# Turning q and the attention's probabilities on VectorE instead of TensorE

## The chip, the cores and the metric

The kernel runs on one core of a Trainium2 chip, in one launch. The metric is device microseconds of an execution. All operands are float32; the products run on values split into two float32r parts.

## The reference

A block with three residual steps on x of 256 tokens by 2048: half a SwiGLU FFN (width 5632), a mixer, and again half a SwiGLU FFN, with an RMSNorm ahead of each and one at the end. The mixer projects to 5376 columns and has two groups of heads:

```python
p = h @ w_in                       # q of 16 heads x 64, k and v of 2 heads x 64, retention's q, k, v, gate
logits = einsum('bnqhgd,bnkhd->bnhgqk', qc, kb) * 64 ** -0.5   # chunks of 64 queries, windows of 128 keys
probs = softmax(concat([logits, sink], -1))[..., :-1]
out = einsum('bnhgqk,bnkhd->bnqhgd', probs, vb)
x = x + concat(out, retention) @ w_out
```

## The kernel before

**Tiling.** The products are weight streams: a weight matrix goes by in groups of 2048 rows by 512 columns (4 MB). A group is eight *halves*; a half is 256 rows, and TensorE computes it in `half` (line 357) as 12 products of 128x512: two row tiles, two token tiles, and three terms each, hi*hi, hi*lo and lo*hi. SP loads 1 MB of weights (two halves) at a time into one of four slots of `raw`. ScalarE copies a half from `raw` into `w_hi` (rounded, line 694), VectorE subtracts to get `w_lo` (line 914). This is a *split*; there are four slots of each, so that a split is made four halves ahead: `position(g, k)` on ScalarE and VectorE is the split of half k + 4, ScalarE's waits until TensorE has finished half k (`half_used`), VectorE's waits for ScalarE's, and TensorE's half waits for VectorE's (`lo_ready`).

**Order.** Every engine runs an order written out by hand; what isn't weight work is put between positions k by `if k == ...`. The input projection has 11 column blocks of up to 512. Two of them, 16 halves, are a *pair*. TensorE's `pair(i, quad)` numbers its halves (e, k) with e = 0, 1 and k = 0 to 7; ScalarE's and VectorE's `in_pair(i, j)` count k = 0 to 15. Pair 0 gives k, v and the first columns of q. The four pairs after it are a loop (`Fori`) in which the attention runs beside the projection, one *quad* (four heads, two token tiles) a pair. The attention is one chain through the engines:

1. GpSimd's `stage` copies the quad's q out of `proj` into `q_in` (line 1207), and k and v into `kT` and `v`; this happens during the quad before.
2. After half 1 TensorE turns q by eight transposes into PSUM (line 392 for every transpose); ScalarE copies to `qT` (line 806).
3. After half 3 the logits (line 512), 32 small products.
4. VectorE takes the maximum in position 3, ScalarE the exponentials into `probs` in position 4 (line 814).
5. After half 8, (1, 0), TensorE turns the probabilities by eight transposes; ScalarE and VectorE copy one bank each to `probsT` (lines 822 and 1101).
6. After half 10, (1, 2), the weighing with v (`weigh`, line 525); VectorE scales by the denominators in position 10 (line 1105), TensorE turns the result after half 13, and both parts of `attT` are made in position 13.

GpSimd, after the last quad's logits, rotates retention's q and k in 24 instructions of 128x512 (`rotate`, lines 1228 to 1235); their scratch is `q_in` and `qT`.

The FFN turns its hidden tile h on VectorE already, by instructions of 32 partitions (`turn_h`, line 983):

```python
out = ps[dst * SQ:(dst + 1) * SQ, B_DOWN:B_DOWN + 2, :].rearrange(
    "p b (j t c) -> p t (b j) c", j=2, t=T)[:, :, :, src * SQ:(src + 1) * SQ]
blocks = h[src * SQ:(src + 1) * SQ, :, :].rearrange(
    "p t (k c) -> p t k c", k=4)[:, :, :, dst * SQ:(dst + 1) * SQ]
m = dve.transpose(out, blocks)
```

Of the kernel before, what the change touches and what calls it, by code (L numbers as in the profile page):

```python
# [20 lines left out]
P = 128  # L21
D = 2048
SEQ = 256
T = SEQ // P
# [9 lines left out]
HD = 64  # L34
KV = 2
QUAD = 4
# [50 lines left out]
def build(nc, x_d, xT_d, g1, u1, d1, w_in, sinks_d, gn_d, w_out, g2, u2, d2, fw_d, ident_d, cos_d, sin_d,  # L87
          decay_d, out_d):
    ffn_w = [(g1, u1, d1), (g2, u2, d2)]
    with ExitStack() as ctx:  # L90
# [3 lines left out]
        def sem(name):  # L94
            return ctx.enter_context(nc.semaphore(name))
# [113 lines left out]
        q_in_ready = sem("q_in_ready")  # L209
        kT_in_ready = sem("kT_in_ready")  # L210
        v_in_ready = sem("v_in_ready")
        q_turned = sem("q_turned")
        qT_ready = sem("qT_ready")
        logits_ready = sem("logits_ready")
        soft = sem("soft")
# [1 line left out]
        sink_m_ready = sem("sink_m_ready")  # L217
        probs_ready = sem("probs_ready")
        sink_e_ready = sem("sink_e_ready")
        probs_turned = sem("probs_turned")  # L220
        probsT_a = sem("probsT_a")
        probsT_b = sem("probsT_b")
        pv_done = sem("pv_done")
        att_ready = sem("att_ready")
        att_turned = sem("att_turned")
# [128 lines left out]
        def _(pe):  # L354
# [160 lines left out]
                mm.then_inc(logits_ready, 1)  # L515

            def weigh(quad):
                pe.wait_ge(probsT_a, quad)
                pe.wait_ge(probsT_b, quad)
                pe.wait_ge(v_in_ready, quad)  # L520
                for t in range(T):
                    for hh in range(QUAD):
                        for c in range(2):
                            col = (t * QUAD + hh) * HD
                            mm = pe.matmul(ps[c * CH:(c + 1) * CH, B_DOWN + 2, col:col + HD],  # L525
                                           probsT[:, t, hh * P + c * CH:hh * P + (c + 1) * CH],
                                           v[:, t, c, :], start=True, stop=True)
                mm.then_inc(pv_done, 1)

            def in_projection():  # L530
                def pair(i, quad=None):
                    for e in range(2):
                        pe.wait_ge(proj_ready, 2 * i + (e + 1))
                        for k in range(8):
                            if quad is None and e == 0:
                                pe.wait_ge(xT_lo_ready, PAIRS * MIX + k + 1)
                            if quad is not None and (e, k) == (0, 3):
                                pe.wait_ge(attT_lo_ready, quad)
                            half(2 * i + (G_IN + e), k, xT_hi, xT_lo, 2 * k, B_GATE + 2 * e, k == 0, k == 7)
                            if quad is None and (e, k) == (1, 2):  # L540
                                pe.wait_ge(proj_ready, 2 + 1)
                                for g in range(KV):
                                    for t in range(T):
                                        mm = turn(B_DOWN, (g * T + t) * P,
                                                  proj[:, t, A_K + g * HD:A_K + (g + 1) * HD])
                                mm.then_inc(k_turned, 1)
                            if quad is not None and (e, k) == (0, 1):
                                pe.wait_ge(kT_ready, 3)
                                pe.wait_ge(q_in_ready, quad)
                                for t in range(T):  # L550
                                    for hh in range(QUAD):
                                        mm = turn(B_DOWN + t, hh * P, q_in[:, t, hh * HD:(hh + 1) * HD])
                                mm.then_inc(q_turned, 1)
                            if quad is not None and (e, k) == (0, 3):
                                logits(quad)
                            if quad is not None and (e, k) == (1, 0):
                                pe.wait_ge(probs_ready, quad)
                                for t in range(T):
                                    for hh in range(QUAD):
                                        mm = turn(B_DOWN + t, hh * P, probs[:, t, hh, :])  # L560
                                mm.then_inc(probs_turned, 1)
                            if quad is not None and (e, k) == (1, 2):
                                weigh(quad)
                            if quad is not None and (e, k) == (1, 5):
                                pe.wait_ge(att_ready, quad)
                                for k2 in range(2):
                                    for t in range(T):
                                        mm = turn(B_DOWN + 3, k2 * SEQ + t * P, att[:, t, k2 * P:(k2 + 1) * P])
                                mm.then_inc(att_turned, 1)

                pair(0)
                with pe.Fori(1, NQ + 1) as quad:
                    pair(quad, quad)
                pe.wait_ge(proj_ready, 2 + NI - 2)
                for k in range(8):
                    half(G_OUT - 1, k, xT_hi, xT_lo, 2 * k, B_GATE, k == 0, k == 7, W_LAST)
# [86 lines left out]
        def _(act):  # L663
# [131 lines left out]
            def in_pair(i, j=None):  # L795
                for k in range(16):
                    position(2 * i + G_IN, k)
                    if k == 7:
                        proj_out(2 * i, B_GATE)
                    if k == 15:  # L800
                        proj_out(2 * i + 1, B_UP)
                    if j is None:
                        continue
                    if k == 1:
                        act.wait_ge(q_turned, j + 1)
                        act.activation(qT.rearrange("p t c -> p (t c)"),
                                       ps[0:HD, B_DOWN:B_DOWN + 2, :].rearrange("p t c -> p (t c)"),
                                       ACT.Copy).then_inc(qT_ready, 1)
                    if k == 4:
                        act.wait_ge(neg_m_ready, j + 1)  # L810
                        for t in range(T):
                            for hh in range(QUAD):
                                c = t * QUAD + hh
                                a = act.activation(probs[:, t, hh, :], ps[:, B_DOWN + 2 + t, hh * P:(hh + 1) * P],
                                                   ACT.Exp, bias=neg_m[:, c:c + 1], scale=HD ** -0.5,
                                                   accum_out=den[:, c:c + 1])
                        a.then_inc(probs_ready, 1)
                        act.wait_ge(sink_m_ready, j + 1)
                        act.activation(sink_e[:], sink_m[:], ACT.Exp).then_inc(sink_e_ready, 1)
                    if k == 8:  # L820
                        act.wait_ge(probs_turned, j + 1)
                        act.activation(probsT[:, 0, :], ps[:, B_DOWN, :], ACT.Copy).then_inc(probsT_a, 1)
                    if k == 13:
                        act.wait_ge(att_turned, j + 1)
                        act.activation(attT_hi[:, bass.ds(2 * j, 2), :], ps[:, B_DOWN + 3, :].rearrange(
                            "p (k s) -> p k s", k=2), ACT.Copy).then_inc(attT_hi_ready, 1)
# [81 lines left out]
        def _(dve):  # L908
# [149 lines left out]
            def weigh_final(t, n):  # L1058

                cols = slice(n * W, (n + 1) * W)  # L1060
                if t == 0 and n < ND - LATE:
                    dve.wait_ge(x_added, X_FFN[1] + 4 * (NF - 1) + n + 1)
                dve.tensor_tensor(normed[:, t, cols], x[:, t, cols], final_w[:, cols],
                                  ALU.mult).then_inc(x_weighted, 1)

            def in_pair(i, j=None):
                for k in range(16):
                    position(2 * i + G_IN, k)
# [7 lines left out]
                                        turned[:, :, 0, CH:2 * CH]).then_inc(kT_ready, 1)  # L1076
                    if j is None:
                        continue
                    if k == 3:

                        dve.wait_ge(logits_ready, j + 1)
# [10 lines left out]
                        dve.wait_ge(neg_m_ready, j + 1)  # L1092
                        dve.tensor_tensor(sink_m[:], sinks[:, bass.ds(8 * j, 8)], neg_m[:],
                                          ALU.add).then_inc(sink_m_ready, 1)
                    if k == 8:
                        dve.wait_ge(sink_e_ready, j + 1)
                        dve.tensor_tensor(den2[:], den[:], sink_e[:], ALU.add).then_inc(soft, 1)
                        dve.wait_ge(soft, 4 * j + 3)
                        dve.reciprocal(rden[:], den2[:]).then_inc(soft, 1)
                        dve.wait_ge(probs_turned, j + 1)  # L1100
                        dve.tensor_copy(probsT[:, 1, :], ps[:, B_DOWN + 1, :]).then_inc(probsT_b, 1)
                    if k == 10:
                        dve.wait_ge(pv_done, j + 1)
                        dve.wait_ge(soft, 4 * j + 4)
                        dve.tensor_tensor(att[:].rearrange("p t (h d) -> p (t h) d", h=QUAD),
                                          ps[:, B_DOWN + 2, :].rearrange("p (h d) -> p h d", d=HD),
                                          rden[:].unsqueeze(2).to_broadcast([P, T * QUAD, HD]),
                                          ALU.mult).then_inc(att_ready, 1)
                    if k == 13:
                        dve.wait_ge(attT_hi_ready, j + 1)  # L1110
                        dve.tensor_tensor(attT_lo[:, bass.ds(2 * j, 2), :],
                                          ps[:, B_DOWN + 3, :].rearrange("p (k s) -> p k s", k=2),
# [81 lines left out]
        def _(pool):  # L1194
# [5 lines left out]
            def stage(j):  # L1200

                again = not isinstance(j, int)
                if again:
                    pool.wait_ge(proj_ready, j + (2 + 1))
                    pool.wait_ge(q_turned, j)
                    pool.wait_ge(v_in_ready, j)
                pool.tensor_copy(q_in[:], proj[:, :, bass.ds(j * QUAD * HD + A_Q, QUAD * HD)]).then_inc(q_in_ready, 1)
                if again:
# [118 lines left out]
```

## Time and profile before

| | us |
|---|---|
| median of 3 runs (lowest, highest) | 1819.68 (1819.52, 1819.89) |
| the profiled execution | 1819.52 |
| its span, first to last instruction | 1817.7 |
| busy: TensorE products / weight loads | 1806.8 / 1495.2 |
| busy: VectorE / ScalarE / GpSimd | 1184.4 / 824.7 / 63.9 |

The span is what the trace shows; 1.8 us of the execution lie around it. Busy time sums the instructions of an engine. A product's record (0.39 us for 128x512) is longer than the distance to the next one, since they are pipelined; for TensorE read distances between starts.

### The profile page before, as it was taken

Reading aid. Unit: us, or ns where it says so; the run is one execution under the profiler, and the core shown is the slowest. Engines: PE = TensorE matmul, PEld = TensorE weight load, DVE = VectorE, ACT = ScalarE, POOL = GpSimd, SP = SyncE. Lnnn points to the kernel's source line nnn. Section 1 sums busy time; section 2 is a strip of 40 time slices with the busy share of each in tenths; the row PEclk is TensorE's granted clock in tenths of the full one; section 3 lists DMA queues with packets and bytes.
Section 4 is the critical chain, followed back from the end, with each engine's and each line's share of the span. In section 5 each row is a group of like instructions: output and inputs, shape, how many; then the busy total and the mean of one; then the engine's idle time right before and its main releaser. Section 6 shows DMA issues by size and latency. Waiting matters only on the chain.

```text
span 1817.7 us, 22705 instructions
## 1 busy us (share of the span) xinstructions
PE 1806.8 (99%) x8308; PEld 1495.2 (82%) x8308; DVE 1184.4 (65%) x1403; ACT 824.7 (45%) x990; POOL 63.9 (4%) x60
## 2 busy tenths in 40 slices
PE   9999999999999999999999999999999999999998
PEld 7888888888888888888888888888888888888886
DVE  6676676676666667544467665676676666667666
ACT  6434444443443444555555455444443443444444
POOL 0000000000000000100045000000000000000000
PEclk9999999999999999999999999999999999999999
DMA  9566566566555555554545456565566555565562
GB/s 384 197 192 201 185 194 198 185 197 195 186 199 192 187 203 186 168 181 163 174 149 185 139 186 208 185 195 198 186 196 196 186 199 192 188 200 190 189 204 93
DMA packets 175587, 346.64 MB, mean 191 GB/s; under 512 B 5952, under 2 KB 8640, under 8 KB 175424
## 3 DMA queue, kind: packets, MB, share of 16 engines
q1 hardware_dynamic: 174976, 345.35, 57.6%
q10 hardware_dynamic: 576, 0.81, 0.1%
q8 instruction: 23, 0.38, 0.1%
q14 instruction: 12, 0.10, 0.0%
HBM read 344.04 MB, written 2.10 MB: 190 GB/s over the span
## 4 chain that ended last, share of the span: by engine, by line
PE 98%; DVE 1%; issue 0%; ACT 0%; DMA 0%; SPq 0%; POOLq 0%; POOL 0%; DVEq 0%; ACTq 0%
PE ps L363 32%; PE ps L365 32%; PE ps L364 32%; PE ps L392 1%; DVE w_lo L914 0%; PE ps L512 0%; DMA raw<-in_g 0%; PE ps L600 0%; PE ps L611 0%; PE ps L525 0%; ACT w_hi L671 0%; ACT w_hi L694 0%; PE ps L481 0%; PE ps L479 0%; PE ps L480 0%
## 5 line engine op out<-in xcount | busy, mean ns | idle before, releaser
L914 DVE TENSOR_TENSOR w_lo<-raw,w_hi 128x1024 fp32r<-128x1024 f32 x644 | 801.3, 1246 | 596.3 <-ACT w_hi L694 595.2
L694 ACT ACTIVATE w_hi<-raw 128x1024 fp32r<-128x1024 f32 x644 | 682.9, 1061 | 962.4 <-PE ps L365 954.1
L363 PE MATMUL ps<-w_hi,xT_hi 128*128 128x512 f32 (+1 forms) x1808 | 703.7, 389 | 1.2 <-DVE w_lo L914 1.1
L365 PE MATMUL ps<-w_hi,xT_lo 128*128 128x512 f32 (+1 forms) x1808 | 700.3, 387 | 0.0
L364 PE MATMUL ps<-w_lo,xT_hi 128*128 128x512 f32 (+1 forms) x1808 | 700.3, 387 | 0.0
L363 PEld LDWEIGHTS ps<-w_hi,xT_hi 128*128 128x128 f32 x1808 | 339.5, 188 | 71.9 <-DVE w_lo L914 1.6
L365 PEld LDWEIGHTS ps<-w_hi,xT_lo 128*128 128x128 f32 x1808 | 339.5, 188 | 69.7
L364 PEld LDWEIGHTS ps<-w_lo,xT_hi 128*128 128x128 f32 x1808 | 339.6, 188 | 68.3
L363 PE MATMUL ps<-w_hi,hT_hi 128*128 128x512 f32 x640 | 249.1, 389 | 0.0
L365 PE MATMUL ps<-w_hi,hT_lo 128*128 128x512 f32 x640 | 249.0, 389 | 0.0
L364 PE MATMUL ps<-w_lo,hT_hi 128*128 128x512 f32 x640 | 249.0, 389 | 0.0
L983 DVE STREAM_TRANSPOSE ps<-h 32x256 f32<-32x256 f32 x320 | 146.0, 456 | 7.1
L365 PEld LDWEIGHTS ps<-w_hi,hT_lo 128*128 128x128 f32 x640 | 120.1, 188 | 25.0
L363 PEld LDWEIGHTS ps<-w_hi,hT_hi 128*128 128x128 f32 x640 | 120.1, 188 | 24.9
L364 PEld LDWEIGHTS ps<-w_lo,hT_hi 128*128 128x128 f32 x640 | 120.1, 188 | 24.8
L999 DVE SCALAR_TENSOR_TENSOR x<-ps,x 128x512 f32<-128x512 f32 x188 | 120.4, 682 | 0.1
L1197 POOL TENSOR_TENSOR rstd<-ms_eps,minus_half 128x2 f32<-128x2 f32 (+1 forms) x5 | 3.2, 641 | 1491.8 <-DVE ms_eps L958 1491.8
L363 PE MATMUL ps<-w_hi,attT_hi 128*128 128x512 f32 x112 | 45.5, 406 | 0.0
L365 PE MATMUL ps<-w_hi,attT_lo 128*128 128x512 f32 x112 | 43.8, 391 | 0.0
L364 PE MATMUL ps<-w_lo,attT_hi 128*128 128x512 f32 x112 | 43.6, 390 | 0.0
L968 DVE SCALAR_TENSOR_TENSOR h<-ps,rstd,sg 128x512 f32<-128x512 f32 x44 | 30.9, 743 | 0.0
L733 ACT ACTIVATE sg<-ps,rstd 128x512 f32<-128x512 f32 x44 | 27.4, 673 | 0.0
(117 smaller groups left out, 522.2 us busy)
## 6 DMA issues: line engine op xcount, KB each, us to landing
raw<-in_u SPq DMA_DIRECT2D x88, 1024.0 KB, 5.1
raw<-in_d SPq DMA_DIRECT2D x88, 1024.0 KB, 4.9
raw<-in_g SPq DMA_DIRECT2D x85, 1024.0 KB, 5.1
raw<-in_w_in SPq DMA_DIRECT2D x40, 1024.0 KB, 4.9
raw<-in_w_out SPq DMA_DIRECT2D x16, 1024.0 KB, 4.9
raw<-in_g SPq DMA_DIRECT2D x4, 512.0 KB, 7.4
x<-in_x SPq DMA_DIRECT2D x4, 512.0 KB, 12.9
raw<-in_w_in SPq DMA_DIRECT2D x4, 512.0 KB, 3.6
```

Of the source, the lines that this page charges most:

```text
L363: pe.matmul(out, xh, wh, start=first and j == 0, stop=False)
L364: pe.matmul(out, xh, wl, start=False, stop=False)
L365: mm = pe.matmul(out, xl, wh, start=False, stop=last and j == 1)
L392: return pe.transpose(ps[0:src.shape[1], bank, col:col + P], src, ident[:])
L694: act.activation(dst, raw[:, s, (k % 2) * HALF:(k % 2 + 1) * HALF], ACT.Copy).then_inc(hi_ready, 1)
L733: act.activation(sg[:, t, :], ps[:, B_GATE + t, :], ACT.Silu, scale=rstd[:, (FFN1, FFN2)[f], t:t + 1]).then_inc(silu_done, 1)
L914: dve.tensor_tensor(w_lo[:, k % LEAD, :, :].rearrange(flat), raw[:, k // 2, (k % 2) * HALF:(k % 2 + 1) * HALF], f32(w_hi[:, k % LEAD, :, : ...
L968: dve.scalar_tensor_tensor(out=h[:, t, :], in0=ps[:, B_UP + t, :], scalar=rstd[:, (FFN1, FFN2)[f], t:t + 1], in1=sg[:, t, :], op0=ALU.mult ...
L983: m = dve.transpose(out, blocks)
L999: a = dve.scalar_tensor_tensor(out=xb, in0=ps[:, B_DOWN + 2 * (n % 2) + t, :], scalar=scale, in1=xb, op0=ALU.mult, op1=ALU.add)
L1197: pool.tensor_tensor(rstd[:, norm, t0:t1], ms_eps[:, norm, t0:t1], minus_half[:, t0:t1], ALU.pow).then_inc(rstd_ready, 1)
```

## The change

Per quad, q is turned by eight and the probabilities by sixteen VectorE transposes, each of which takes 32 partitions by 256 elements (eight blocks of 32x32) from one group of 32 partitions of the source and writes them to a group of `qT` or `probsT`. TensorE's sixteen transposes, ScalarE's copies to `qT` and `probsT` and VectorE's to `probsT` go. Three transposes follow each of VectorE's positions 0 and 1, two position 2 (q), four follow positions 6 and 7, three 8 and 9, two 10 (probabilities). On TensorE the weighing moves from after half 10 to after half 11 and the turn of its result from half 13 to half 14; VectorE's denominators move from position 8 to 11, the scaling from 10 to 12, the making of `attT` from 13 to 14. GpSimd's next `q_in` waits for `qT_ready` where it waited for `q_turned`.

```diff
@@ TensorE
             def weigh(quad):
-                pe.wait_ge(probsT_a, quad)
-                pe.wait_ge(probsT_b, quad)
+                pe.wait_ge(probsT_ready, quad)
@@
-                            if quad is not None and (e, k) == (0, 1):
-                                pe.wait_ge(kT_ready, 3)
-                                pe.wait_ge(q_in_ready, quad)
-                                for t in range(T):
-                                    for hh in range(QUAD):
-                                        mm = turn(B_DOWN + t, hh * P, q_in[:, t, hh * HD:(hh + 1) * HD])
-                                mm.then_inc(q_turned, 1)
                             if quad is not None and (e, k) == (0, 3):
                                 logits(quad)
-                            if quad is not None and (e, k) == (1, 0):
-                                pe.wait_ge(probs_ready, quad)
-                                for t in range(T):
-                                    for hh in range(QUAD):
-                                        mm = turn(B_DOWN + t, hh * P, probs[:, t, hh, :])
-                                mm.then_inc(probs_turned, 1)
-                            if quad is not None and (e, k) == (1, 2):
+                            if quad is not None and (e, k) == (1, 3):
                                 weigh(quad)
-                            if quad is not None and (e, k) == (1, 5):
+                            if quad is not None and (e, k) == (1, 6):
                                 pe.wait_ge(att_ready, quad)
@@ ScalarE
-                    if k == 1:
-                        act.wait_ge(q_turned, j + 1)
-                        act.activation(qT.rearrange("p t c -> p (t c)"),
...
-                    if k == 8:
-                        act.wait_ge(probs_turned, j + 1)
-                        act.activation(probsT[:, 0, :], ps[:, B_DOWN, :], ACT.Copy).then_inc(probsT_a, 1)
-                    if k == 13:
+                    if k == 14:
                         act.wait_ge(att_turned, j + 1)
@@ VectorE
+            def turn_q(b0, b1):
+                for b in range(b0, b1):
+                    d, c = b // 4, b % 4
+                    to = qT_full[d * SQ:(d + 1) * SQ, :, :].rearrange("p t (h c) -> p t h c", h=QUAD)
+                    of = q_in[c * SQ:(c + 1) * SQ, :, :].rearrange("p t (h c) -> p t h c", h=QUAD)
+                    m = dve.transpose(to[:, :, :, c * SQ:(c + 1) * SQ], of[:, :, :, d * SQ:(d + 1) * SQ])
+                return m
+            def turn_probs(b0, b1):
+                for b in range(b0, b1):
+                    d, c = b // 4, b % 4
+                    to = probsT[d * SQ:(d + 1) * SQ, :, :].rearrange("p t (h c) -> p t h c", h=QUAD)
+                    of = probs[c * SQ:(c + 1) * SQ, :, :, :]
+                    m = dve.transpose(to[:, :, :, c * SQ:(c + 1) * SQ], of[:, :, :, d * SQ:(d + 1) * SQ])
+                return m
@@ in_pair
+                    if k == 0:
+                        dve.wait_ge(q_in_ready, j + 1)
+                    if k < 3:
+                        m = turn_q(3 * k, min(3 * k + 3, 8))
+                    if k == 2:
+                        m.then_inc(qT_ready, 1)
@@
-                    if k == 8:
+                    if k == 6:
+                        dve.wait_ge(probs_ready, j + 1)
+                    if 6 <= k < 11:
+                        m = turn_probs(*((0, 4), (4, 8), (8, 11), (11, 14), (14, 16))[k - 6])
+                    if k == 10:
+                        m.then_inc(probsT_ready, 1)
+                    if k == 11:
                         dve.wait_ge(sink_e_ready, j + 1)
...
-                        dve.wait_ge(probs_turned, j + 1)
-                        dve.tensor_copy(probsT[:, 1, :], ps[:, B_DOWN + 1, :]).then_inc(probsT_b, 1)
-                    if k == 10:
+                    if k == 12:
                         dve.wait_ge(pv_done, j + 1)
...
-                    if k == 13:
+                    if k == 14:
                         dve.wait_ge(attT_hi_ready, j + 1)
@@ GpSimd
-                    pool.wait_ge(q_turned, j)
+                    pool.wait_ge(qT_ready, j)
```

## Rows read from the trace of the kernel before

**Rows 1.** The page, chain that ended last: share of the span by engine.

```profile
PE 98%; DVE 1%; issue 0%; ACT 0%; DMA 0%; SPq 0%; POOLq 0%; POOL 0%; DVEq 0%; ACTq 0%
```

**Rows 2.** Waits, 770 to 970 us: engine, line, releaser; us in total, times, longest.

```profile
PEld ps L512 <- issue: 1.4, 4, 0.4
```

**Rows 3.** Windows, one pair: length, busy us (instructions) by engine, clock, DMA share, GB/s.

```profile
778.50:827.77 49.27, 49.27 (x278) 40.64 (x276) 23.48 (x25) 25.20 (x42) 3.66 (x3) 1.00 0.52 171
```

**Rows 4.** Timeline of PE in the first quad: start, length, engine, line, operation, operands.

```profile
778.49 0.40 PE L365 MATMUL ps<-w_hi,xT_lo 128*128 128x512 f32 x1
...
782.11 0.39 PE L365 MATMUL ps<-w_hi,xT_lo 128*128 128x512 f32 x1
...
784.83 0.39 PE L365 MATMUL ps<-w_hi,xT_lo 128*128 128x512 f32 x1
785.15 1.96 PE L512 MATMUL ps<-kT,qT 64*64 64x64 f32 x32
...
800.59 0.39 PE L365 MATMUL ps<-w_hi,xT_lo 128*128 128x512 f32 x1
...
804.21 0.39 PE L365 MATMUL ps<-w_hi,xT_lo 128*128 128x512 f32 x1
...
806.93 0.39 PE L365 MATMUL ps<-w_hi,xT_lo 128*128 128x512 f32 x1
807.25 1.15 PE L525 MATMUL ps<-v,probsT 128*64 128x64 f32 x32
```

**Rows 5.** VectorE in the FFN: group (count, busy us, mean ns), then its timeline.

```profile
L983 DVE STREAM_TRANSPOSE ps<-h 32x256 f32<-32x256 f32 x320 | 146.0, 456 | 7.1
...
301.01 1.23 DVE L914 TENSOR_TENSOR w_lo<-raw,w_hi 128x1024 fp32r<-128x1024 f32 x1 [1.49 <-ACT w_hi L694]
302.15 1.28 DVE L999 SCALAR_TENSOR_TENSOR x<-ps,x 128x512 f32<-128x512 f32 x2
...
314.70 1.23 DVE L914 TENSOR_TENSOR w_lo<-raw,w_hi 128x1024 fp32r<-128x1024 f32 x1 [0.38 <-ACT w_hi L694]
315.96 0.91 DVE L983 STREAM_TRANSPOSE ps<-h 32x256 f32<-32x256 f32 x2
```

**Rows 6.** Groups of VectorE by shape: two-input and one-input work within SBUF.

```profile
L1063 DVE TENSOR_TENSOR proj<-x,proj 128x512 f32<-128x512 f32 x8 | 5.3, 689 | 0.2
...
L1190 DVE TENSOR_SCALAR proj<-proj,rstd 128x512 f32<-128x512 f32 x3 | 1.3, 484 | 0.7 <-POOL rstd L1197 0.7
```

**Rows 7.** Timelines of ACT and DVE at the head of the first quad's pair.

```profile
776.27 1.28 ACT L694 ACT_TABLE_LOAD   x1 [0.58 <-PE ps L365]
...
778.93 1.06 ACT L694 ACTIVATE w_hi<-raw 128x1024 fp32r<-128x1024 f32 x1 [0.30 <-PE ps L365]
...
778.66 2.59 DVE L914 TENSOR_TENSOR w_lo<-raw,w_hi 128x1024 fp32r<-128x1024 f32 x2 [2.86 <-ACT w_hi L694]
```

**Rows 8.** Timelines of ACT and DVE around the first quad's probabilities.

```profile
798.30 1.06 ACT L694 ACTIVATE w_hi<-raw 128x1024 fp32r<-128x1024 f32 x1 [1.66 <-PE ps L365]
...
801.02 1.06 ACT L694 ACTIVATE w_hi<-raw 128x1024 fp32r<-128x1024 f32 x1 [0.51 <-PE ps L365]
...
796.68 1.22 DVE L914 TENSOR_TENSOR w_lo<-raw,w_hi 128x1024 fp32r<-128x1024 f32 x1 [0.30 <-ACT w_hi L694]
799.39 1.23 DVE L914 TENSOR_TENSOR w_lo<-raw,w_hi 128x1024 fp32r<-128x1024 f32 x1 [1.49 <-ACT w_hi L694]
```

**Rows 9.** The last quad: line 914 (min/median/max ns), then DVE, POOL and PE timelines.

```profile
L914 DVE TENSOR_TENSOR w_lo<-raw,w_hi x7: 1257/2002/2360, 939.2 to 956.3; 128x1024 fp32r<-128x1024 f32 x7
...
943.00 6.46 DVE L914 TENSOR_TENSOR w_lo<-raw,w_hi 128x1024 fp32r<-128x1024 f32 x3 [1.48 <-ACT w_hi L694]
...
944.00 2.16 POOL L1228 TENSOR_TENSOR q_in<-proj,sin 128x512 f32<-128x512 f32 x1
...
955.09 1.15 PE L525 MATMUL ps<-v,probsT 128*64 128x64 f32 x32
```

**Rows 10.** Timeline of PE: its first instructions of the run.

```profile
1.46 3.60 PE L625 MATMUL ps<-junk 128*128 128x512 bf16 x8 [1.46 <-DVE junk L1116]
```

More of the change, by code:

```diff
@@ L211, in build @@
         v_in_ready = sem("v_in_ready")
-        q_turned = sem("q_turned")
         qT_ready = sem("qT_ready")
@@ L219, in build @@
         sink_e_ready = sem("sink_e_ready")
-        probs_turned = sem("probs_turned")
-        probsT_a = sem("probsT_a")
-        probsT_b = sem("probsT_b")
+        probsT_ready = sem("probsT_ready")
         pv_done = sem("pv_done")
@@ L803, in in_pair @@
                         continue
-                    if k == 1:
-                        act.wait_ge(q_turned, j + 1)
-                        act.activation(qT.rearrange("p t c -> p (t c)"),
-                                       ps[0:HD, B_DOWN:B_DOWN + 2, :].rearrange("p t c -> p (t c)"),
-                                       ACT.Copy).then_inc(qT_ready, 1)
                     if k == 4:
```

## The prediction

> **What bounds the kernel now.** I read the chain of waits first: 98% of what ended last is TensorE [rows 1]. Then the waits of the stage that the change touches: no other engine holds TensorE there, only its own issue, as the 1.4 us ahead of the four quads' logits [rows 2]. Then the same stage by windows: one pair of column blocks lasts 49.27 us and TensorE is busy for all of it at granted clock 1.00 (2.4 GHz), while VectorE is busy for 23.48 us and ScalarE for 25.20 us [rows 3]. So an instruction taken from TensorE is worth its full time, and one added to VectorE is free only until TensorE waits for its result.
>
> **What TensorE gives back.** A half is 12 products of 128x512. An undisturbed one goes from 782.11 to 784.83, 2.72 us. The half before it, with the eight transposes of q in front, goes from 778.49 to 782.11, 3.62 us: 0.90 us for the eight and the disturbance behind them. The probabilities' eight: 800.59 to 804.21, 3.62 us, again 0.90 us, and the half after it 2.72 us [rows 4]. 2 x 0.90 = 1.80 us a quad, 7.2 us for four quads. ScalarE also loses two copies and VectorE one; both were behind work that nobody waited for, so I count them at nothing.
>
> **What VectorE gets: the price of one transpose.** The trace has the same instruction, 32x256 float32, but from SBUF into PSUM: 456 ns, 320 times [rows 5]; the new ones write SBUF. Bounds: a two-input SBUF instruction of 128x512 takes 689 ns and a one-input one 484 ns [rows 6], so one-input SBUF work can stream two elements a cycle of about 1.04 ns. If the new transposes did, 256 elements would cost 133 ns less. From above, 484 ns is 267 ns of that faster streaming and 217 ns fixed, and 217 + 267 for 256 elements at one a cycle is again 484 ns. I take 456 ns, the same operation, and keep 0.32 and 0.484 us as ends.
>
> How closely they follow each other matters as much. A split of 128x1024 (record 1.23 us) is followed by an ordinary instruction after 1.14 us (301.01 to 302.15), but by a transpose that goes to other partitions after 1.26 us (314.70 to 315.96), and a pair of transposes takes 0.91 us, twice 456 ns with no overlap [rows 5]. So 0.456 us each in a chain, against 0.34 us if starts overlapped by the same 0.12 us.
>
> The Trainium skill, "VectorE: DVE Perf Modes", section "Two Vector instructions with no wait between them", has this as a rule: an instruction whose input or output starts in another group of 32 partitions than the last one is held until all earlier ones have finished. The trace agrees (1.26 against 1.14 us); by the rule nearly all 24 new transposes and the splits behind them are held, and without it they would not be, which is a rival below. The same page, section "The three transpose paths", gives 311 ns for a 128x128 bf16 transpose into SBUF; an estimate from it for twice the elements, at 0.96 GHz, is 311 + 133 = 444 ns, by which the sum below would be about 0.8 us smaller.
>
> **The q turn: does it fit?** Position k of VectorE is the split for the half four later; it needs ScalarE's w_hi, whose start VectorE's follows by 1.09 us (798.30, 799.39 [rows 8]). At the loop's head ScalarE reloads its table (1.28 us at 776.27), so VectorE's position 0 starts late, at 778.66, and position 1's input is there at 778.93 + 1.09 = 780.02 [rows 7]. Now the new queue: split at 778.66, first transpose after 1.14 (it stays on the first partitions), three of 0.456 end at 781.17; split 1.26 and three more end at 783.80; split 1.26 and two end at 785.97. Every split's input is there before its turn. TensorE reached the logits at 785.15 [rows 4]; without the q turn it is there at 784.25. It waits 1.72 us plus 0.1 us for signal and start (my estimate): 1.8 us a quad, twice what the q transposes gave back. Behind the waiting TensorE stands half 4, then everything. ScalarE and the DMAs only follow; weight loads have the lead of four halves, 10.9 us. VectorE's next work, position 3 and the maximum, waits for the logits anyway, and GpSimd's q_in copy, now released by the same signal, falls beside that split: nothing for either.
>
> **The probabilities' turn.** Times as in the trace before, counted from the logits. Position 6 starts at 796.68 [rows 8], the exponentials being done. +1.14 and four transposes: 799.64. Position 7's input was there at 799.39; 1.26 + 1.82: 802.72. Position 8's (801.02 + 1.09 = 802.11) is there; 1.26 + 1.37: 805.35. Positions 9 and 10 are also late by VectorE itself: +1.26 + 1.37 = 807.98, +1.26 + 0.91 = 810.15. TensorE weighed at 807.25, after half 10; now it does so after half 11 and without the turn: 807.25 - 0.90 + 2.72 = 809.07. Wait: 1.08 + 0.1 = 1.2 us a quad. The VectorE copy and den2/rden moved to position 11 lie behind it; att at 12 and its turn after half 14 keep over 1 us of room; no w_lo is late, since half 11's is made at 800.9 for a start at about 806.
>
> **The last quad.** Once its logits are done GpSimd rotates, 24 instructions on end. There the splits take 2.00 us in the median and three in a row 6.46 us, and GpSimd's instructions 2.16 us where they meet one [rows 9]. Two-input SBUF instructions of both take turns; the transposes have one input, and I leave them at 0.456. Position 5 ends at 943.00 + 2.15 = 945.15; five splits of 2.00 and 16 transposes are 17.3 us: 962.45. TensorE is there at 955.09 - 0.90 + 2.72 = 956.91, counted in the same way. Wait: 5.5 + 0.1 = 5.6 us in place of 1.2.
>
> **Sum.** -7.2 + 4 x 1.8 + 3 x 1.2 + 5.6 = +9.2 us. The profiled execution took 1819.52 us (span 1817.7), 0.16 below the median of 1819.68. Forecast 1819.5 + 9.2 = 1828.7 us, 0.5% slower. Its own range: transposes of 0.484 add 2.7 us, five splits of 2.36 (the longest of that row [rows 9]) 1.8; gentler turns with GpSimd take off up to 4.4.
>
> **Rivals.**
> 1. GpSimd doesn't lengthen the last turn (the transposes let it run in their time): the last wait is 1.2 us too, +4.8 us, 1824.3. For it: GpSimd's instructions alone are short; against it: it has 24 of them in a row, so some one is under way whenever a split comes.
> 2. The starts overlap (no hold): 0.34 us each. q wait 0.9; the second is then paced by ScalarE, about 0.35; the last 945.15 + 10.0 + 5.4 + 0.1 - 956.9 = 3.8. -7.2 + 3.6 + 1.05 + 3.8 = +1.2 us: 1820.7, no change. Against it: the 1.26 us of rows 5.
> 3. The other side: transposes from SBUF to SBUF stream two elements a cycle and overlap, 0.34 - 0.13 = 0.21 us. Then VectorE has q ready at about 784.3 and the probabilities at 809.1, waits of 0.1 us, and the last about 1.5 us: -7.2 + 0.4 + 0.3 + 1.5 = -5.0 us, 1814.5. It decides from the spacing below which the waits sum to under 7.2 us, about 0.32 us. For it: the 484 ns of rows 6; against it: 456 ns in 320 transposes, though none of them could show it, having PSUM as target.
> 4. The clock. It is 1.00 through this stage before [rows 3], but TensorE never idles there. The first eight 128x512 products of the run, after nothing, take 3.60 us, 0.42 us apart [rows 10], where 0.227 is the spacing at 2.4 GHz: the lower level, 1.2 GHz. If the last wait of 5.6 us brings it back for as many products, that is 8 x 0.2 = 1.6 us more, 1830.3. The Trainium skill, "TensorE: Matmul & The Clock Gate", section "Why this matters for your kernels", warns of this for idle gaps; no row here shows it.
>
> **Chances.** Forecast 0.46, with the clock's extra 0.09, rival 1 0.2, rival 2 0.12, rival 3 0.08, something else 0.05. The likeliest one's time is the prediction. The range 1820.3 to 1833.5 holds rivals 1, 2 and 4 and the dearer transposes. 0.2% (3.6 us) is about what a measurement of this kernel can tell from no change. Slower: forecast, clock and rival 1 save a small part of it, 0.73; the same: rival 2 and that part, 0.16; faster: rival 3 and half of the rest, 0.11.
>
> **What would show it.** TensorE waits ahead of the logits, named VectorE, four times 1.8 us; ahead of weigh, 1.2 us three times and over 4 us in the last quad; pairs of 49.27 - 1.80 + 3.0 = 50.5 us; new transposes of 440 to 485 ns, back to back; clock 1.00 but for the last quad. I am wrong if the transposes are under 0.35 us apart, if a w_lo is waited for, or if the waits are there but TensorE's transposes had cost less than 0.90 us a turn.

## The result, and the profile after

The changed kernel takes 1834.27 us (median of 4, 1830.99 to 1836.11) against 1819.79: ratio 1.0078, 95% interval 1.0064 to 1.0091. It is slower by 14.5 us; the forecast of 1828.7 us is 8.9 above this median, and the upper end of its range, 1833.5, was passed by 0.8 us. The profiled execution took 1834.15 us, span 1832.3.

The chain that ended last, against [rows 1]: TensorE has lost three parts in a hundred of it to VectorE and to "issue".

```profile
PE 95%; DVE 2%; issue 2%; ACT 0%; POOLq 0%; POOL 0%; DVEq 0%; ACTq 0%
```

Who waited for whom, 770 to 990 us, against [rows 2] (engine, line waited; us in total, times, longest; PEld is the weight load that waits, PE the product behind it; line 509 is the logits, 521 weigh, 1054 the transposes of the probabilities):

```profile
PEld ps L521 <- DVE probsT L1054: 9.9, 4, 5.8
PEld ps L509 <- issue: 8.2, 4, 2.1
PE ps L521 <- DVE probsT L1054: 8.2, 4, 5.4
PE ps L509 <- issue: 6.7, 4, 1.7
```

Both waits of the prediction are there, four times each: up to 1.7 us ahead of each logits, and ahead of weigh 0.94 us three times and 5.4 once. The one ahead of the logits is called "issue": this view doesn't name its releaser, and the timeline of VectorE has to be laid beside it. The timeline of TensorE in the first quad, against [rows 4], and in the last, against [rows 9]:

```profile
783.96 0.39 PE L362 MATMUL ps<-w_hi,xT_lo 128*128 128x512 f32 x1
786.01 0.65 PE L509 MATMUL ps<-kT,qT 64*64 64x64 f32 x12 [1.66 <-issue]
```

```profile
809.56 0.39 PE L362 MATMUL ps<-w_hi,xT_lo 128*128 128x512 f32 x1
810.88 0.80 PE L521 MATMUL ps<-v,probsT 128*64 128x64 f32 x20 [0.94 <-DVE probsT L1054]
```

```profile
966.42 0.39 PE L362 MATMUL ps<-w_hi,xT_lo 128*128 128x512 f32 x1
972.16 1.12 PE L521 MATMUL ps<-v,probsT 128*64 128x64 f32 x16 [5.35 <-DVE probsT L1054]
```

VectorE at the head of the first quad, against [rows 7]:

```profile
778.69 1.23 DVE L889 TENSOR_TENSOR w_lo<-raw,w_hi 128x1024 fp32r<-128x1024 f32 x1 [2.86 <-ACT w_hi L677]
779.83 1.32 DVE L1046 STREAM_TRANSPOSE qT<-q_in 32x256 f32<-32x256 f32 x3
781.16 1.23 DVE L889 TENSOR_TENSOR w_lo<-raw,w_hi 128x1024 fp32r<-128x1024 f32 x1
782.42 1.33 DVE L1046 STREAM_TRANSPOSE qT<-q_in 32x256 f32<-32x256 f32 x3
783.76 1.23 DVE L889 TENSOR_TENSOR w_lo<-raw,w_hi 128x1024 fp32r<-128x1024 f32 x1
785.02 0.89 DVE L1046 STREAM_TRANSPOSE qT<-q_in 32x256 f32<-32x256 f32 x2
```

The queue is the one that was worked out: the last q transpose ends at 785.91 (785.97 was forecast) and the logits start at 786.01. The new transposes against [rows 5]:

```profile
L1054 DVE STREAM_TRANSPOSE probsT<-probs 32x256 f32<-32x256 f32 x64 | 27.9, 436 | 1.1
...
L1046 DVE STREAM_TRANSPOSE qT<-q_in 32x256 f32<-32x256 f32 x32 | 13.9, 434 | 0.5
```

436 and 434 ns, 0.02 us less than those into PSUM, one behind the other without overlap (three in 1.32 to 1.33 us), and 1.26 us from a split's start to a first transpose that goes to other partitions, 1.14 to one that doesn't. That is the hold of [rows 5].

What the forecast lacks stands in the windows (length, busy us of PE, clock, DMA share, GB/s) behind the second quad's q wait:

```profile
836.00:838.00 2.00, 1.82 (x26) 0.70 0.56 216
838.00:840.00 2.00, 2.00 (x12) 0.50 0.63 136
840.00:842.00 2.00, 2.00 (x7) 0.50 0.99 386
842.00:844.00 2.00, 2.00 (x7) 0.60 0.01 2
844.00:846.00 2.00, 2.00 (x11) 1.00 0.00 0
```

The granted clock falls to 0.50, the 1.2 GHz level, while the logits run behind the 1.66 us of idleness (their 32 small products have 64x64 on one side and 64 or 128 columns on the other), and is back at 2.4 GHz before 844. Products are then 0.43 us apart in place of 0.227:

```profile
840.26 0.63 PE L362 MATMUL ps<-w_hi,xT_lo 128*128 128x512 f32 x1
840.69 0.63 PE L360 MATMUL ps<-w_hi,xT_hi 128*128 128x512 f32 x1
```

**The account**, by the start of the first logits product and of the first weigh product in each quad. The column on the right is the run fill, described below, whose TensorE has work in the waits. Undisturbed, logits to weigh would be 22.10 - 0.90 + 2.72 = 23.92 us.

| us | before | after | after, TensorE kept busy (fill, below) |
|---|---|---|---|
| logits to weigh, quad 1 | 22.10 | 24.87 | 24.90 |
| quad 2 | 22.10 | 28.07 | 24.89 |
| quad 3 | 22.10 | 26.47 | 24.90 |
| quad 4 | 22.10 | 30.86 | 29.49 |
| weigh to the next logits | 27.18 | 25.29 to 25.30 | 25.30 to 25.33 |
| last weigh to the retention's first transpose | 31.37 | 28.92 | 26.85 |

Weigh to logits is 27.18 - 2.72 - 0.90 + 1.74: the q wait is 1.74 us. The last line would be 31.37 - 2.72 = 28.65; fill has 1.8 us less, because the kernel before waited there and fill doesn't. The projection's last group is narrow (256 columns), its splits took turns with GpSimd's rotation, and TensorE waited for w_lo (kernel before, 965 to 1003 us, line 914):

```profile
PEld ps L363 <- DVE w_lo L914: 1.6, 3, 0.7
```

In the changed kernel and in fill the rotation, started by the logits, is over earlier against TensorE, which has waited ahead of weigh; that view of them has no such row. The changed kernel loses 28.92 - 26.85 = 2.07 us there all the same, at clock 0.50, which it reached within its last weigh wait of 5.35 us (0.50 from 970 on):

```profile
972.00:974.00 2.00, 1.84 (x32) 0.50 0.00 0
974.00:976.00 2.00, 2.00 (x9) 0.50 0.66 173
976.00:978.00 2.00, 2.00 (x9) 0.82 0.25 89
```

So: give-back -7.2; q waits 4 x 1.74 = 7.0; weigh waits 3 x 0.95 = 2.9; the last weigh wait 29.49 - 23.92 = 5.6; the clock, by the differences between after and fill, 3.18 + 1.57 + 1.37 + 2.07 = 8.2; the narrow group's wait -1.8. Sum +14.7; the spans differ by 14.6.

The four runs say the same by their mean clock: 1830.99 us at 0.996, 1834.15 and 1834.38 at 0.993, 1836.11 at 0.992. A varying number of falls would explain the scatter of 5 us in a kernel whose predecessor scatters by 0.6; only one of the four was profiled.

### The profile page after: what moved, and what is told of

Its sections match the earlier page's. It is cut to its first block, busy times and chain, and to the rows that moved or that the text cites. A ratio compares the mean times of both kernels' runs of the same rounds, so it can differ in the third digit from the quotient of the medians.

```text
span 1832.3 us, 22657 instructions
## 1 busy us (share of the span) xinstructions
PE 1807.8 (99%) x8244; PEld 1496.2 (82%) x8244; DVE 1217.2 (66%) x1495; ACT 819.0 (45%) x982; POOL 57.3 (3%) x60
## 4 chain that ended last, share of the span: by engine, by line
PE 95%; DVE 2%; issue 2%; ACT 0%; POOLq 0%; POOL 0%; DVEq 0%; ACTq 0%
PE ps L360 31%; PE ps L361 31%; PE ps L362 31%; DVE probsT L1054 1%; DVE w_lo L889 1%; PE ps L389 1%; PE ps L509 1%; PE ps L521 0%; ACT w_hi L677 0%; PE ps L583 0%; PE ps L594 0%; PE ps L380 0%; PE ps L376 0%; PE ps L384 0%; PE ps L608 0%
## 5 line engine op out<-in xcount | busy, mean ns | idle before, releaser
L1054 DVE STREAM_TRANSPOSE probsT<-probs 32x256 f32<-32x256 f32 x64 | 27.9, 436 | 1.1
```

The costliest lines, as they stand in the source:

```text
L1054: m = dve.transpose(to[:, :, :, c * SQ:(c + 1) * SQ], of[:, :, :, d * SQ:(d + 1) * SQ])
```

## The experiments

Theory: the 14.5 us are give-back, two waits and the clock falls behind them. Rivals: VectorE's work beside TensorE costs by itself; or the clock has another cause. Ratios are against the kernel before, whose median was 1819.6 to 1819.9 us beside these runs.

**q_only**: the probabilities' half of the change undone.

```diff
-                        m = turn_probs(*((0, 4), (4, 8), (8, 11), (11, 14), (14, 16))[k - 6])
...
+                            if quad is not None and (e, k) == (1, 0):
...
+                                        mm = turn(B_DOWN + t, hh * P, probs[:, t, hh, :])
...
```

> Only the q turn is VectorE's; the probabilities are turned by TensorE and weighed after half 10, as before. Theory (the waits, and clock falls behind the q waits): TensorE gives back 4 x 0.90 = 3.6 us and waits 4 x 1.73 = 6.9 us ahead of the logits, +3.3 us over the kernel before (1819.8), so 1823.1 at full clock; and 1.2 to 1.7 us more for each quad in which the clock falls behind the wait (in the changed kernel three of four), so about 1827 and a mean clock near 0.996. Rival (the clock falls behind the long last weigh wait or the number of VectorE transposes, not behind the q waits): 1823 with clock 0.999.

Measured 1828.60 us (1828.33 to 1829.86), ratio 1.0052 (1.0038 to 1.0066), clock 0.995. The same q waits, and the fall behind the second:

```profile
PEld ps L511 <- issue: 8.2, 4, 2.1
PE ps L511 <- issue: 6.6, 4, 1.7
```

```profile
832.00:842.00 10.00, 8.34 (x51) 0.75 0.62 208
842.00:852.00 10.00, 10.00 (x41) 0.91 0.01 2
```

Logits to weigh is 22.05, 25.28, 23.67 and 23.62 us: 3.2 + 1.6 + 1.5 us above 22.10. The falls belong to the q waits; the rival would have had 1823. The time is 1.6 us above the theory's 1827, since the falls cost 6.3 us together where it had at most 5.1. The account closes: -3.6 + 7.0 + 6.3, and -0.8 for the last weigh to the retention (30.56 us against 31.37), is +8.9.

**probs_only**: the q half undone.

```diff
-                        m = turn_q(3 * k, min(3 * k + 3, 8))
...
+                                        mm = turn(B_DOWN + t, hh * P, q_in[:, t, hh * HD:(hh + 1) * HD])
...
```

> Only the probabilities are VectorE's; q is turned by TensorE after half 1. Theory: -3.6 us, weigh waits of 0.95 us in three quads and about 5.2 in the last, +4.4 us: 1824.2 at full clock, with one fall, in the last quad behind its wait, 1.6 to 3 us more: 1825.8 to 1827, clock 0.998, and no fall at 1 us waits. Rival (falls come with VectorE's transposes beside TensorE anywhere): clock under 0.996 and over 1828.

Measured 1825.35 us (1824.81 to 1825.74), ratio 1.0031 (1.0019 to 1.0044), clock 0.997: the mechanism as the theory had it, the time 0.4 us under its range. Logits to weigh is 24.93 us in three quads, with no fall behind their waits, and 29.59 in the last, behind which the clock is 0.70 in the mean of 10 us. The halves, +8.9 and +5.6, add up to the +14.5. That is in part luck: their falls come to 8.5 us where the changed kernel's come to 8.2, and what they save in the narrow group to 2.6 where it saves 1.8.

**fill**: TensorE is kept busy in the waits. What the fillers compute is used by nobody.

```diff
+            def fill(n):
+                for _ in range(n):
+                    pe.matmul(ps[:, B_DOWN + 1, :], xT_hi[:, 0, 0:P], xT_hi[:, 0:2, :].rearrange("p k s -> p (k s)"),
+                              start=True, stop=True)
...
+                                fill(6)
                                 logits(quad)
...
+                                fill(20 if isinstance(quad, int) else 3)
                                 weigh(quad)
...
-                with pe.Fori(1, NQ + 1) as quad:
-                    pair(quad, quad)
+                with pe.Fori(1, NQ) as quad:
+                    pair(quad, quad)
+                pair(NQ, NQ)
```

> The changed kernel with products of x by itself into an unused bank ahead of each wait, 6 ahead of the logits (1.36 us of the 1.73 waited), 3 ahead of weigh, 20 in the last quad (4.5 us); their results are used by nobody. Theory: the waits end when they did, since VectorE sets their end, but TensorE isn't idle: clock back to 0.999 and the time to the sum of give-back and waits alone, 1819.8 - 7.2 + 6.9 + 2.9 + 5.2 = 1827.6. Rival (the clock isn't part of it, the 14.5 us are all waits): 1834 or, since the fillers add work, more.

Measured 1826.04 us (1825.78 to 1826.15), ratio 1.0035 (1.0021 to 1.0048), clock 0.999. More work on TensorE made it 8.2 us faster, and its runs agree within 0.4 us. The logits start at 786.01 and 836.24, where the changed kernel's do (786.01, 836.18): VectorE still sets them. TensorE's last pair also stands outside the loop here, for its 20 fillers; the second and third quads, in the loop in both kernels, lose their falls all the same (28.07 and 26.47 us against 24.89 and 24.90). The second quad's window in the changed kernel, then in fill:

```profile
822.00:872.00 50.00, 47.40 (x245) 38.75 (x244) 31.54 (x47) 22.12 (x38) 2.52 (x3) 0.93 0.50 166
```

```profile
822.00:872.00 50.00, 49.44 (x270) 40.58 (x269) 33.03 (x49) 23.65 (x40) 2.53 (x3) 1.00 0.50 168
```

The 8.2 us are the clock's share of the account, and all of it. It ended 1.6 us under the theory, which lacked the narrow group's wait (1.8 us) and had 5.2 for a last wait of 5.6.

**early_q**: the same eight transposes, in positions 11 to 15 of the pair before.

```diff
+                    if turn_next and k == 11:
+                        dve.wait_ge(q_in_ready, done + 1)
+                    if turn_next and k >= 11:
+                        m = turn_q(*((0, 2), (2, 3), (3, 5), (5, 6), (6, 8))[k - 11])
+                    if turn_next and k == 15:
+                        m.then_inc(qT_ready, 1)
...
-                    if k < 3:
-                        m = turn_q(3 * k, min(3 * k + 3, 8))
...
```

> The changed kernel with each quad's q turned one pair earlier, in VectorE's positions 11 to 15; same instructions, no wait at the logits. Theory: the 6.9 us of q waits and the falls behind them go; left are -7.2 + 2.9 + 5.2 = +0.9 us and one fall in the last quad, 1.6 to 3 us: 1822 to 1824, clock 0.998. Rival (VectorE's load beside TensorE costs, wherever it is put): over 1828.

Measured 1821.69 us (1821.00 to 1822.62), ratio 1.0011 (1.0002 to 1.0020), clock 0.997: 12.6 us back for moving eight instructions a quad, and 0.3 us under the theory's range. What is left ahead of the logits is the 1.4 us of issue of [rows 2]; weigh's waits stand:

```profile
PEld ps L521 <- DVE probsT L1054: 10.1, 4, 6.0
PE ps L521 <- DVE probsT L1054: 8.4, 4, 5.6
...
PEld ps L509 <- issue: 1.4, 4, 0.4
```

**early_q_alone**: q as in early_q, the probabilities as before.

> Only q is VectorE's, turned one pair earlier; the probabilities are turned by TensorE as before. Theory: half of the give-back and no wait, -3.6 us: 1816.1, clock 0.999. Rival (VectorE's eight transposes delay a w_lo or the give-back is less): 1818 or more.

Measured 1816.05 us (1815.76 to 1816.90), ratio 0.9981 (0.9972 to 0.9990): the half give-back to 0.1 us. Logits to weigh is 22.09 us, weigh to logits 26.28, that is 27.18 - 0.90: a turn costs TensorE 0.90 us, and eight transposes a quad beside it cost it nothing.

**late_rotate**: the changed kernel with GpSimd held until the last weighing.

```diff
-            pool.wait_ge(logits_ready, NQ)
+            pool.wait_ge(pv_done, NQ)
```

> The changed kernel, but GpSimd's rotation waits for the last quad's weighing instead of its logits. Theory: the last weigh wait shrinks from about 5.2 us to the 0.95 of the other quads, 4.2 us, and the one clock fall behind it goes, about 1.3 us: 1834.3 - 5.5 = 1828.8, clock 0.995, the q waits and their falls left. Rival (the last wait is long for another reason, or the rotation is then late for the retention): 1833 or more.

Measured 1833.79 us (1833.36 to 1835.39), ratio 1.0079 (1.0065 to 1.0092). The total is the rival's, though the last wait did shrink: its longest weigh wait is 1.4 us. Its clock falls ahead of weigh (26.43, 28.06, 26.47, 26.43 us from logits to weigh) are 7.9 us above four times 24.87, where the changed kernel has 6.1. Its trace also has two waits behind the last weighing that the changed kernel's lacks, 1.9 us for w_lo in and right behind the narrow group and 1.9 us for `att` in the retention. The next run has the same two, without clock falls.

**early_q_late_rotate**: early_q and late_rotate together.

> q turned one pair earlier and the rotation late; all 24 transposes a quad still VectorE's. Theory: left are the give-back and four weigh waits of 0.95 us, -7.2 + 3.8 = -3.4 us: 1816.3, clock 0.999, faster than the kernel before. Rival (transposes beside TensorE cost it something by themselves): 1818 or more.

Measured 1820.42 us (1819.97 to 1821.63), ratio 1.0006 (0.9997 to 1.0015), clock 0.999: not to be told from no change, and a miss by 4.1 us. The wait is gone as expected (early_q has 10.1 us, longest 6.0, in this row):

```profile
PEld ps L521 <- DVE probsT L1054: 5.4, 4, 1.4
```

Logits to weigh in the last quad is 24.91 us, as in the others, where early_q has 29.59: the last wait was GpSimd's doing, 4.7 us of it. The total is the rival's (1818 or more), its mechanism isn't: 24 transposes a quad run beside TensorE, and weigh to logits is 23.56 to 23.60 us where 27.18 - 2.72 - 0.90 = 23.56 was due. The gain was given back later: TensorE waits 1.9 us for w_lo in and right behind the narrow group (1.6 before, in the narrow group) and 1.9 us for `att` in the retention. The next run shows the second at its clearest.

**no_waits**: as the last one, and weigh after half 12.

```diff
-                            if quad is not None and (e, k) == (1, 3):
+                            if quad is not None and (e, k) == (1, 4):
                                 weigh(quad)
...
```

> As the one with early q and late rotation, and weigh one half later again (after half 12, the scaling in position 13, attT in 15): no wait left. Theory: the whole give-back, -7.2 us: 1812.5, clock 0.999. Rival (a dependent step of the last quad is then late, or the give-back was less than 0.90 us a turn): 1814 or more.

Measured 1821.12 us (1820.69 to 1821.86), ratio 1.0009 (0.9999 to 1.0018). A miss by 8.6 us, and the first half of the rival (a dependent step of the last quad is late) is what happened. No quad waits (26.64 us from logits to weigh, 23.92 + 2.72), but the retention does:

```profile
PE ps L389 <- ACT att L849: 4.4, 1, 4.4
PE ps L360 <- DVE w_lo L889: 2.3, 4, 0.6
```

`gn_rstd` is the scale of a retention head's norm, which GpSimd computes behind all four rotations in its order. GpSimd still rotates when the first head's is due; ScalarE's `att` waits for it, and TensorE waits 4.4 us for ScalarE. In that wait the clock falls, and it is 0.50 from 1002 to 1008. It is a new wait, made by my own edit.

**split_rotate**: the changed kernel with only heads 1 to 3 of the rotation held.

```diff
             for hd in range(RH):
+                if hd == 1:
+                    pool.wait_ge(pv_done, NQ)
                 rotate(hd)
```

> The changed kernel, with GpSimd rotating head 0 behind the last logits as it did, and heads 1 to 3 behind the last weighing. The late rotation of all four heads ended too late for the retention's first gn_rstd (TensorE waited there instead); this one should end some 8 us earlier. Theory: the last weigh wait becomes 0.95 us, its clock fall goes, no new wait: 1834.3 - 4.2 - 1.3 = 1828.8. Rival (the last wait isn't GpSimd's doing, or the retention waits anyway): 1833 or more.

Measured 1832.78 us (1831.08 to 1834.25), ratio 1.0069 (1.0056 to 1.0083). It missed by 4 us, at the edge of the rival's 1833: the four weigh waits are alike (5.4 us in all), but in the profiled execution the clock fell in every quad (28.10, 26.48, 26.47, 28.09 us from logits to weigh, 9.7 us above four times 24.87), and the narrow group waits again (1.7 us for w_lo). Where the q waits stand, a gain of 4 us can't be read from the total.

**split_no_waits**: early q, weigh after half 12, split rotation.

> q turned one pair earlier, weigh after half 12, and the rotation split in the same way. Theory: no wait at the logits, at weigh or in the retention: the whole give-back of 16 transposes a quad, 1819.6 - 7.2 = 1812.4, clock 0.999. Rival (GpSimd still ends too late, or transposes beside TensorE cost it something): 1815 or more.

Measured 1814.46 us (1814.04 to 1814.97), ratio 0.9970 (0.9959 to 0.9982), clock 0.999: the fastest, 5.4 us under the kernel before, of 7.2 expected. For the missing 1.8 us the trace shows GpSimd again: it rotates through the whole narrow group, nine splits take 19.59 us, 2.2 each, and TensorE's halves wait for w_lo (line 889). The median is under the rival's 1815. From weigh to the retention it is 27.07 us where 31.37 - 2 x 2.72 = 25.93 were to be had, and the retention's first head takes 0.7 us longer:

```profile
966.68 19.59 DVE L889 TENSOR_TENSOR w_lo<-raw,w_hi 128x1024 fp32r<-128x1024 f32 x9
```

```profile
PE ps L360 <- DVE w_lo L889: 2.0, 4, 0.6
```

## Why the prediction was wrong

- **Give-back, 7.2 us**: right. early_q_alone and the pairs of starts give 0.90 us a turn.
- **Price of a transpose, 0.456 us, held**: right in kind, 0.436 in size. (For 444 ns the prediction has the sum about 0.8 us smaller; 96 transposes of 12 ns less are 1.2 us, as its own 2.7 us for 484 ns is 96 times 28 ns.) The overlap of rival 2 and the doubled stream of rival 3 aren't there.
- **q wait, 1.8 us**: 1.74. **Weigh wait, 1.2 us**: 0.95, since the 16 transposes ahead of it are 20 ns shorter each. **The last one, 5.6 us**: 5.6. GpSimd as its cause is shown by early_q against early_q_late_rotate; rival 1 is out.
- **Missed**: the narrow group's wait of the kernel before, 1.8 us, which goes. It stands in that trace, behind the stage that the prediction read.
- With these the sum would be -7.2 + 7.0 + 2.9 + 5.6 - 1.8 = +6.5 us, 1826.0 at the profiled execution; fill, which has the waits without the falls, takes 1826.04.
- **The step that failed is the clock.** The forecast's sum has it at nothing, and rival 4 gave it a chance of 0.09 and 1.6 us, once, behind the last wait, because I took the longest wait to be the dangerous one. It took 8.2 us: 3.2 in the second quad, 1.6 in the third, 1.4 in the fourth's first part, 2.1 behind the last weigh wait. fill shows it: same ends of the waits, TensorE busy in them, clock 0.999, 8.2 us less. q_only shows where: behind the q waits of 1.7 us, while the waits of 0.95 us ahead of weigh brought no fall in any profile here. Whether the longer wait or the smaller products behind it make that difference isn't shown, since the two go together.
- The Trainium skill, "TensorE: Matmul & The Clock Gate", section "Why this matters for your kernels", warns that idle gaps between products cost the clock, and speaks of longer gaps than the q waits. The trace agrees for the wait of 5.35 us, and shows falls behind waits of 1.66 us as well. I cited it and still priced it for one wait out of eight.
- The whole miss, 5.5 us at the profiled execution, is smaller than the clock's 8.2 because the other terms were 2.7 us too high together. That is luck: the eight waits had been read nearly right, what the clock does behind them had not.
- The profile's name for the q wait was "issue", not VectorE, as I had said it would be.

Not tried: why the clock falls in one quad and not in another of the same execution, as in the first quad of the changed kernel, whose q wait is also 1.66 us.

## What to carry to other kernels

Moving work off the bounding engine pays only if its new home delivers before the old time: write the receiving engine's queue out, instruction by instruction, from its late start at a loop's head, and give the result another stage of lead first (here 12.6 us for moving eight transposes into the pair before). When TensorE is made to wait, price the clock at every such wait and not only at the longest (here 6.1 of the 8.2 us came ahead of weigh, behind waits of 1.7 us), and look at the scatter of the runs. And an engine held back to end one contention needs its later consumers checked: its order is a queue too.

## What the runs showed of the hardware

- TensorE, idle for 1.66 us and then in the small products of the logits, fell to 1.2 GHz in three or four of the four such places of an execution (after and q_only three, late_rotate and split_rotate four); kept busy by fillers it fell in none. The same small products with no wait ahead of them, in the kernel before, brought no fall.
- A 32x256 float32 transpose from SBUF to SBUF takes 436 ns on VectorE, 456 into PSUM, and isn't slowed by GpSimd: in the last quad four took 1.77 us as elsewhere, while the splits between them, with two inputs in SBUF, took 1.65 to 2.10 in place of 1.23:

```profile
957.22 1.77 DVE L1054 STREAM_TRANSPOSE probsT<-probs 32x256 f32<-32x256 f32 x4
959.00 1.79 DVE L889 TENSOR_TENSOR w_lo<-raw,w_hi 128x1024 fp32r<-128x1024 f32 x1
960.83 1.78 DVE L1054 STREAM_TRANSPOSE probsT<-probs 32x256 f32<-32x256 f32 x4
962.62 1.65 DVE L889 TENSOR_TENSOR w_lo<-raw,w_hi 128x1024 fp32r<-128x1024 f32 x1
964.31 1.34 DVE L1054 STREAM_TRANSPOSE probsT<-probs 32x256 f32<-32x256 f32 x3
965.66 2.10 DVE L889 TENSOR_TENSOR w_lo<-raw,w_hi 128x1024 fp32r<-128x1024 f32 x1
```
